# Memory keys and values in three fp32r products; the second norm's scale ahead of the third row pair; GpSimd adds the fourth pair too

## Chip, cores and metric

The kernel runs on one core of a Trainium2 chip, as one program. The metric is the device time of an execution in microseconds; lower is better. TensorE (PE) multiplies, VectorE (DVE), ScalarE (ACT) and GpSimd (POOL) work on tiles in SBUF and PSUM, and SyncE (SP) issues nearly all DMAs.

## What is computed

One layer of a streaming encoder for 512 prompt tokens and 64 sample tokens (T = 576), D = 1024. Three branches (convolution, latent attention, attention into a memory) are gated, summed, projected and normed; a mixture of 32 experts (one group of four, two of its eight experts per token) and a second norm follow. Cut to what matters here:

```python
proj = x @ w_in        # GLU input | q latent | kv latent + rotary key | memory queries | gates
mem_k = (mem_prompt @ w_mem_k).reshape(n_p, n_mem, MEM_HEADS, MEM_HEAD_DIM)   # 256 memory tokens, 4 heads of 128
mem_v = (mem_prompt @ w_mem_v).reshape(n_p, n_mem, MEM_HEADS, MEM_HEAD_DIM)
y_mem = mem_attend(mem_q, mem_k, mem_v)                # softmax(q k / sqrt(128)) v
merged = gates[0] * y_conv + gates[1] * y_mla + gates[2] * y_mem
x1 = layer_norm(DEEPNORM_ALPHA * x + merged @ w_out, g_ln1, b_ln1)
y = hier_moe(x1, ...)                                  # sum of two weighted experts per token
x2 = layer_norm(DEEPNORM_ALPHA * x1 + y, g_ln2, b_ln2)
```

## The kernel before

The program is written by hand, engine by engine: each engine has one list of instructions that it works off in order, and waits on semaphores. A tensor is kept with features on the partitions and tokens along the row.

**Products in three fp32r parts.** The projections of x (weights of 1024 x 128, one "job" each) aren't multiplied in plain fp32. Of a weight item, ACT makes the high part (`high_parts`, L1205; fp32r copy, L1214) and DVE or POOL the low part (`low_part`, L506; subtraction, L512); PE forms high x high, high x low of x, low x high (`product`, L746; matmuls L757). A job on 576 tokens has 8 x 3 x 2 = 48 matmuls of 288 columns. `SPLIT` (L96) lists the items treated like this. They sit in two buffers, `WH[n % 2]` and `WL[n % 2]`; ACT makes part n when the job of part n - 2 is done. `LOW_BY_DVE` (L504) says whose low part DVE makes; POOL makes the others. In the stretch in question these are all DVE's, and POOL has no arithmetic from 17 to 225 us.

**Order of the first stage on PE.** Eight GLU jobs, q0 to q2, kv0, kv1, mq0 to mq3 (memory queries), then kr (rotary key, L801, plain fp32, from `x_raw`). Then plain fp32 again: memory key mk0 (L740, 8 matmuls of 256 columns, `memT` moving), kr_sum (L818), mk1, the sums of squares q_ss and kv_ss (L770), mk2, mk3. Then the memory values: mv_0 to mv_3, each two of eight contraction blocks, 16 matmuls of 512 columns in all (L836); ahead of mv_3 four score products of the memory attention (L781). After that come 20 units of memory attention (4 heads, 5 token tiles): per unit scores, row maximum on DVE (L1589), exponent on ACT (L1282), normalising on DVE (L1596, L1597), two turns on PE (L852), their copy on ACT (L1270), values on PE (L872). The first turn also waits until ACT has moved both value tiles out of PSUM (L1304). Accumulation uses four pairs of PSUM banks; job i takes the pair of job i - 4 (`PAIR`, `BEFORE`, L74) and waits until that one is read.

**Order on DVE.** With each job DVE makes one low part and then seven taps of the convolution (L1522: a product with a scalar and an add, input and accumulator both in SBUF, 576 elements; 124 in all). After mq3's low part come three adds (L1554 to L1556) of squares, 26 taps (7 of the list and 19, L1558), the wait for the root that ACT takes of q_ss (L1256), a reciprocal (L1560), three products, a second reciprocal (L1566) and four products, the rotary key (L1576 to L1580), and then the row maxima of the memory attention, with a tap after every second unit.

**Loads.** Weight items run through a ring of three slots of 1024 columns (`ring`, `ITEMS`, L84); SP loads item i when item i - 3 is released (`released`, L481): by its low part if it is split, by its last use on PE otherwise.

**The tail.** An expert stage gathers rows, multiplies and scatters results; the last three stages stay on the chip as `late_hi` and `late_lo` (L1446, L1885) and are added by one-hot matmuls (L1188). Both expert rows of a token tile come back from DRAM as a pair (`yab`, L689). For tiles 0 and 1 (`N_PAIRED`) POOL adds the pair (L2145), for tiles 2 to 4 PE adds the second row by an identity product (L1179). DVE adds both to the sum (L1976, one input from PSUM), ACT takes variance and root (L1487 to L1491), DVE norms with `lnbc_2` (L1987, L1988), SP writes out (L717). Scale and bias of this norm are loaded ahead of the fifth pair (L687), behind a wait for `e_y`, because an expert's weights lay in their place.

Of the kernel before, what the change touches and what calls it, by code (L numbers as in the profile page):

```python
# [21 lines left out]
D = 1024  # L22
# [64 lines left out]
ITEMS += [(n, 1024, n) for n in ("q0", "q1", "q2", "kv0", "kv1", "mq0", "mq1", "mq2", "mq3")] + [("kr", 256, "kr")]  # L87
# [8 lines left out]
SPLIT = [n for n, _, _ in ITEMS if n != "kr" and n[0] != "u" and n[:2] not in ("mk", "mv")]  # L96
SP_AT = {n: i for i, n in enumerate(SPLIT)}

# [31 lines left out]
N_PAIRED = 2  # L130
# [19 lines left out]
def program(nc, a, o):  # L150

    ctx = ExitStack()
    with ctx:
# [81 lines left out]

        branch = {"z": zT, "om": omT, "ox": oxT}
# [244 lines left out]
        def released(name):  # L481

            if name in SP_AT:
                return (w_lo, SP_AT[name] + 1)
            if name[:3] == "mv_" and name != "mv_3":
                return (mv_used, int(name[3:]) + 1)
            return (job_done, JOB[ITEMS[ITEM[name]][2]] + 1)

# [30 lines left out]
        def _(sp):  # L519
# [205 lines left out]
        def _(pe):  # L725
# [20 lines left out]
            def product(name, it, xh, xl, nk, at=0, first=False, cols=(HT, HT)):  # L746
# [5 lines left out]
                for k in range(nk):  # L752
                    if first:
                        pe.wait_ge(x_lo, k + 1)
                    for w, x in ((WH, xh), (WH, xl), (WL, xh)):
                        for s in range(2):
                            mm = pe.matmul(half(name, s, 128, cols[s]), w[:, n % 2, at + 128 * k:at + 128 * k + 128],  # L757
                                           x[:, k, t0[s]:t0[s] + cols[s]],
                                           start=(k == 0 and w is WH and x is xh), stop=(k == nk - 1 and w is WL))
# [33 lines left out]
            for name in ("q0", "q1", "q2", "kv0", "kv1", "mq0", "mq1", "mq2", "mq3"):  # L793
                proj(name)
# [8 lines left out]
            mm.then_inc(job_done, 1)  # L803
            pe.wait_ge(const_ready, 4)
            pe.wait_ge(in_mem, 48)

            def mem_key(h):
                w = item(f"mk{h}").rearrange("p (k m) -> p k m", k=KT)
                gemm(f"mk{h}", w, lambda k, s: memT[:, k, :], KT, n=MT, halves=1)

            for h in range(MH):
                mem_key(h)
                if h == 0:
                    begin("kr_sum")
                    pe.wait_ge(fold_ready, 1)
                    pe.wait_ge(kr_read, 1)
                    for s in range(2):
                        mm = pe.matmul(half("kr_sum", s, ROPE), fold[:, :], rp[:, 2, HT * s:HT * s + HT], start=True, stop=True)  # L818
                    mm.then_inc(job_done, 1)
                if h == 1:  # L820
                    pe.wait_ge(lat_sum, 2)
                    total("q_ss", 1, sq)
                    total("kv_ss", 1, rp)
            begin("mv0")
            begin("mv1")
            for i in range(4):
# [5 lines left out]
                w = item(f"mv_{i}").rearrange("p (k n) -> p k n", k=2)  # L832
# [339 lines left out]
            for tt in range(NT):  # L1172
# [3 lines left out]
                if tt >= N_PAIRED:  # L1176
# [4 lines left out]
                for n in range(N_LATE):  # L1181
                    if tt == 0:
                        pe.wait_ge(late_rows, 2 * n + 2)
                    for part in (late_hi[n], late_lo[n]):
                        if tt == 0 and part is late_lo[n]:
                            pe.wait_ge(e_yb, N_OUT + n + 1)
                        for h in range(2):
                            mm = pe.matmul(late_bank(tt)[0:nr, h, :], row_hot[:, n, t0:t0 + nr], part[:, 512 * h:512 * h + 512],  # L1188
                                           start=(tt < N_PAIRED and n == 0 and part is late_hi[n]),
# [5 lines left out]
        def _(act):  # L1195
# [9 lines left out]
            def high_parts(upto):  # L1205

                while parts[0] <= SP_AT[upto]:
# [6 lines left out]
                    act.activation(WH[:, n % 2, 0:size], ring[:, i % RING, 0:size], ACT.Copy).then_inc(w_hi, 1)  # L1214
# [24 lines left out]
            for h in range(MH):  # L1239
                if h < 2:  # L1240
                    high_parts(f"mq{h + 2}")
                wait_job(act, f"mq{h}")
                act.activation(split(memq[:, h, :]), both(f"mq{h}"), ACT.Copy, scale=MD ** -0.5).then_inc(mem_proj, 1)
            act.wait_ge(const_ready, 4)
            wait_job(act, "kr")
            act.activation(split(rp[:, 2, :]), both("kr"), ACT.Copy).then_inc(kr_read, 1)

            for h in range(MH):
                wait_job(act, f"mk{h}")
                act.activation(mkT[:, 0, h, :], half(f"mk{h}", 0, 128, MT), ACT.Copy).then_inc(mem_proj, 1)  # L1250
                if h == 0:
                    wait_job(act, "kr_sum")
                    act.activation(split(rp[0:32, 2, :]), both("kr_sum", 32), ACT.Copy).then_inc(kr_read, 1)
                if h == 1:
                    wait_job(act, "q_ss")
                    act.activation(split(norms[:, 0, :]), both("q_ss"), ACT.Sqrt, bias=eps[:, :], scale=1.0 / QL).then_inc(lat_std, 1)  # L1256
                    wait_job(act, "kv_ss")
# [987 lines left out]
```

## Time and profile before

| | |
|---|---|
| median of 3 runs | 859.07 us (857.51 to 860.6) |
| profiled execution | 858.51 us, span 855.6 us |
| PE busy | 793.8 us, 93% |
| DVE, ACT, POOL busy | 44%, 28%, 19% |
| DMA | 172.44 MB, 202 GB/s over the span; 422 to 425 GB/s in most slices from 640 us |
| granted TensorE clock, mean | 0.972 of full speed |

The page gives for each engine the busy time over the whole span, and the same in 40 slices. A share over the span says little about one stage: DVE is at 44% in the mean and at 9 tenths in several slices between 43 and 128 us. So the views that count are the chain of waits (work followed back from the last instruction), the timelines of single engines, and the busy time in chosen stretches. A matmul on fp32 data stands in the records as two, so counts of plain products are doubled there; the last instruction of a group also shows its way through the array (0.3 us), so the distance between starts is the better price.

### The profile page before, as it was taken

What the parts mean: (1) busy time and instruction counts of PE and PEld (TensorE: products, weight loads), DVE (VectorE), ACT (ScalarE), POOL (GpSimd) and SP (SyncE); (2) the same over time, 40 slices, a digit from 0 to 9 for tenths busy, and PEclk for the clock granted to TensorE, in tenths of its full rate; (3) what the DMA queues carried; (4) which work ended last, traced back from release to release, by engine and by line L of the source; (5) the groups of instructions that cost most, each with busy time, mean ns of one, the idle gap of its engine ahead of it and who ended that gap; (6) DMA issues with size and microseconds to landing.
All of it is one profiled execution on the core that took longest, in us unless ns stands there. A gap on an engine that the chain in (4) does not pass through costs nothing.

```text
span 855.6 us, 12244 instructions
## 1 busy us (share of the span) xinstructions
PE 793.8 (93%) x4884; PEld 581.7 (68%) x4884; DVE 375.0 (44%) x676; ACT 239.4 (28%) x463; POOL 160.7 (19%) x160
## 2 busy tenths in 40 slices
PE   5999999999899999999999999998899989786894
PEld 5999986775465999999999994776333333222242
DVE  4799997866676421011101115657321111111227
ACT  5123312744677622122212232011111000000132
POOL 5000001000411343444344330002101011011020
PEclk9999999999999999999999999999899989998798
DMA  8433224213100463222221209659899999999993
GB/s 320 138 103 97 65 75 148 87 47 62 49 2 1 154 207 97 87 67 82 99 87 62 87 1 386 238 208 402 324 388 422 422 424 424 421 425 423 422 386 124
DMA packets 33427, 172.44 MB, mean 202 GB/s; under 512 B 6350, under 2 KB 6910, under 8 KB 25048
## 3 DMA queue, kind: packets, MB, share of 16 engines
q1 hardware_dynamic: 28888, 161.30, 49.6%
q0 software_dynamic: 4480, 10.34, 3.2%
q8 instruction: 39, 0.64, 0.3%
q14 instruction: 20, 0.16, 0.1%
HBM read 162.07 MB, written 15.20 MB: 207 GB/s over the span
## 4 chain that ended last, share of the span: by engine, by line
PE 73%; DMA 18%; DVE 4%; issue 2%; SPq 2%; ACT 1%; POOL 0%; POOLq 0%; ACTq 0%; DVEq 0%
PE PS L757 40%; DMA expert<-in_w_e 7%; PE PS L960 7%; DMA x_rows<-rows,tabs 6%; PE PS L1093 6%; PE PS L740 5%; PE PS L872 3%; PE PS L785 2%; DMA lnbc<-in_b_ln 2%; PE PS L852 2%; PE PS L836 2%; PE PS L916 1%; SPq L689 1%; DMA rows<-x_rows,tabs 1%; PE PS L1117 1%
## 5 line engine op out<-in xcount | busy, mean ns | idle before, releaser
L757 PE MATMUL PS<-x_hi,w_hi 128*128 128x288 f32 (+2 forms) x656 | 142.0, 298 | 9.9 <-DVE x_lo L1505 9.0
L757 PE MATMUL PS<-x_lo,w_hi 128*128 128x288 f32 (+2 forms) x656 | 141.5, 298 | 0.0
L757 PE MATMUL PS<-x_hi,w_lo 128*128 128x288 f32 (+2 forms) x656 | 141.3, 297 | 0.0
L1093 PE MATMUL PS<-expert,moe_tmp 128*64 128x512 f32 (+2 forms) x576 | 113.1, 635 | 12.8 <-DMA expert<-in_w_e 11.3
L1214 ACT ACTIVATE w_hi<-raw_ring 128x1024 fp32r<-128x1024 f32 (+1 forms) x57 | 57.1, 1001 | 214.4 <-PE PS L757 208.5
L757 PEld LDWEIGHTS PS<-x_hi,w_hi 128*128 128x128 f32 x656 | 106.2, 191 | 10.2 <-POOL w_lo L512 9.0
L757 PEld LDWEIGHTS PS<-x_lo,w_hi 128*128 128x128 f32 x656 | 106.3, 191 | 0.0
L757 PEld LDWEIGHTS PS<-x_hi,w_lo 128*128 128x128 f32 x656 | 106.3, 191 | 0.0
L512 POOL TENSOR_TENSOR w_lo<-raw_ring,w_hi 128x1024 fp32r<-128x1024 f32 (+1 forms) x33 | 70.1, 2124 | 136.2 <-ACT w_hi L1214 136.2
L1522 DVE SCALAR_TENSOR_TENSOR conv_z<-attn_tmp,wdw,conv_z 128x576 f32<-128x576 f32 x120 | 90.6, 814 | 0.3
L1093 PEld LDWEIGHTS PS<-expert,moe_tmp 128*64 128x64 f32 (+2 forms) x576 | 35.9, 135 | 78.3 <-issue 76.4
L1660 DVE TENSOR_TENSOR attn_tmp<-attn_tmp,PS 128x576 f32<-128x576 f32 x24 | 18.1, 754 | 148.7 <-PE PS L757 148.7
L1117 PE MATMUL PS<-expert,moe_tmp 128*32 128x512 f32 (+2 forms) x272 | 56.0, 656 | 3.6 <-DMA expert<-in_w_e 3.6
L1869 DVE TENSOR_TENSOR moe_tmp<-moe_tmp,PS 128x256 f32<-128x256 f32 x15 | 6.3, 422 | 106.7 <-ACT moe_tmp L1414 106.7
L512 DVE TENSOR_TENSOR w_lo<-raw_ring,w_hi 128x1024 fp32r<-128x1024 f32 x24 | 30.4, 1268 | 48.3 <-ACT w_hi L1214 47.9
L1117 PEld LDWEIGHTS PS<-expert,moe_tmp 128*32 128x32 f32 (+2 forms) x272 | 16.2, 138 | 33.6 <-issue 33.6
L1414 ACT ACTIVATE moe_tmp<-PS 128x256 f32<-128x256 f32 x15 | 5.8, 384 | 117.2 <-PE PS L1093 117.2
L1589 DVE TENSOR_REDUCE nb<-PS 128x1 f32<-128x256 f32 (+5 forms) x60 | 27.8, 464 | 20.5 <-PE PS L785 13.3
L2102 POOL DMA_INDIRECT rows<-x_rows,tabs x12 | 12.1, 1009 | 128.6 <-DMA x_rows<-rows,tabs 112.7
L1890 DVE SCALAR_TENSOR_TENSOR rows<-PS,w_slot,rows 128x1024 f32<-128x1024 f32 x12 | 15.4, 1284 | 43.3 <-PE PS L1117 43.3
L1043 PE MATMUL PS<-ident,rows 128*128 128x128 f32 x120 | 18.0, 298 | 15.6 <-DMA rows<-x_rows,tabs 12.1
L1043 PEld LDWEIGHTS PS<-ident,rows 128*128 128x128 f32 x120 | 14.2, 150 | 27.0 <-DMA rows<-x_rows,tabs 17.2
(343 smaller groups left out, 1178.2 us busy)
## 6 DMA issues: line engine op xcount, KB each, us to landing
expert<-in_w_e SPq DMA_DIRECT2D x30, 2048.0 KB, 25.2
expert<-in_w_e SPq DMA_DIRECT2D x34, 1024.0 KB, 25.1
raw_ring<-in_w_gate_t SPq DMA_DIRECT2D x24, 512.0 KB, 3.5
raw_ring<-in_w_glu_t SPq DMA_DIRECT2D x8, 512.0 KB, 4.7
raw_ring<-in_w_como_t SPq DMA_DIRECT2D x8, 512.0 KB, 3.6
heads<-in_w_out SPq DMA_DIRECT2D x1, 4096.0 KB, 13.8
x_rows<-x_tiles SPq DMA_DIRECT2D x8, 512.0 KB, 5.4
expert_out<-x_rows SPq DMA_DIRECT2D x8, 512.0 KB, 16.0
```

What stands on the lines that cost most here:

```text
L512: eng.tensor_tensor(WL[:, n % 2, 0:size], ring[:, i % RING, 0:size], WH[:, n % 2, 0:size].bitcast(F32), ALU.subtract).then_inc(w_lo, 1)
L740: mm = pe.matmul(half(name, s, m, n), w[:, k, :], rhs(k, s), start=(k == 0), stop=(k == nk - 1))
L757: mm = pe.matmul(half(name, s, 128, cols[s]), w[:, n % 2, at + 128 * k:at + 128 * k + 128], x[:, k, t0[s]:t0[s] + cols[s]], start=(k == 0 ...
L872: mm = pe.matmul(PS[r * w:(r + 1) * w, 4 + g % 2, 128 * c:128 * c + nr], v, PT[kind][0:nk, n % 4, 128 * j:128 * j + nr], start=(j == 0), s ...
L960: mm = pe.matmul(PS[r0:r0 + nr, 2 * (PAIR[f"c{tt}"]) + s, :], m, w[:, 512 * s:512 * s + 512], start=(k == 0 and n == 0), stop=(k == KT - 1 ...
L1043: mm = pe.transpose(PS[:, k // 4, 128 * (k % 4):128 * (k % 4) + CAP], xg[b][0:CAP, 128 * k:128 * k + 128], ident[0:CAP, 0:CAP])
L1093: mm = pe.matmul(PS[r0:r0 + nr, 2, :].rearrange("p (s f) -> p s f", s=2), xgT[:, k, r0:r0 + nr], w13[s % NB][:, :, k, :], start=(k == 0), ...
L1117: mm = pe.matmul(banks[r0:r0 + nr, h, :], turned[:, j, r0:r0 + nr], w2[s % NB][:, j, 512 * h:512 * h + 512], start=(j == 0), stop=(j == 1))
L1214: act.activation(WH[:, n % 2, 0:size], ring[:, i % RING, 0:size], ACT.Copy).then_inc(w_hi, 1)
L1522: ins = dve.scalar_tensor_tensor(dst, src, wdw[:, c, j:j + 1], dst, ALU.mult, ALU.add)
L1589: dve.tensor_reduce(nb[0:nr, n % 8:n % 8 + 1], PS[0:nr, S_BANK[n % 4], 0:nk], AX.X, ALU.max, negate=True).then_inc(max_done, 1)
L1660: dve.tensor_tensor(split(gate[:, j % 2, n, :]), split(gate[:, j % 2, n, :]), both(f"{name}_{j}"), ALU.mult).then_inc(gate_mul, 1)
```

## The change

Keys and values of the memory are computed like the projections, in three fp32r products. The memory gets a high part `MEM_HI` (ACT, one 128 x 2048 copy) and a low part `MEM_LO` (POOL, one subtraction in place of `memT`). The eight weight items mk0 to mk3 and mv_0 to mv_3 join `SPLIT`: ACT makes their high parts, POOL their low parts (`low_parts("mv_3")`, ahead of its latent outputs). During these eight a third weight buffer is in use (`WH2`, `WL2`; `W_BUF`, `W_PREV`), in the region of `x_raw`. Therefore kr, which reads `x_raw`, moves ahead of mq0, and kr_sum, q_ss and kv_ss move ahead of mk0. In the tail, g_ln2 is loaded ahead of the third pair and b_ln2 ahead of the fourth, and POOL adds the fourth pair (`PAIRED = (0, 1, 3)`).

```diff
@@ jobs and items
-JOBS += ["q0", "q1", "q2", "kv0", "kv1", "mq0", "mq1", "mq2", "mq3", "kr",
-         "mk0", "kr_sum", "mk1", "q_ss", "kv_ss", "mk2", "mk3", "mv0", "mv1"]
+JOBS += ["q0", "q1", "q2", "kv0", "kv1", "kr", "mq0", "mq1", "mq2", "mq3",
+         "kr_sum", "q_ss", "kv_ss", "mk0", "mk1", "mk2", "mk3", "mv0", "mv1"]
...
-SPLIT = [n for n, _, _ in ITEMS if n != "kr" and n[0] != "u" and n[:2] not in ("mk", "mv")]
+SPLIT = [n for n, _, _ in ITEMS if n != "kr" and n[0] != "u"]
 SP_AT = {n: i for i, n in enumerate(SPLIT)}
+W_BUF = {SP_AT["mk0"] + i: 2 - i % 3 for i in range(8)}
+W_BUF = {n: W_BUF.get(n, n % 2) for n in range(len(SPLIT))}
+W_PREV = {n: max((p for p in range(n) if W_BUF[p] == W_BUF[n]), default=None) for n in W_BUF}
...
-N_PAIRED = 2
+PAIRED = (0, 1, 3)
@@ SP, tail
             for tt in range(NT):
                 t0, nr = TILES[tt]
-                if tt == NT - 1:
+                if 2 <= tt < 4:
                     sp.wait_ge(e_y, STAGE_OF[LAST_OF_4] + 1)
-                    for n, name in enumerate(("g_ln2", "b_ln2")):
-                        sp.dma_start(lnbc_2[:, n, :], a[name].broadcast_to([128, D])).then_inc(in_ln, 16)
+                    sp.dma_start(lnbc_2[:, tt - 2, :], a["b_ln2" if tt == 3 else "g_ln2"].broadcast_to([128, D])).then_inc(in_ln, 16)
@@ PE (kr and the sums ahead, as in JOBS)
             for h in range(MH):
-                mem_key(h)
...
+                n = SP_AT[f"mk{h}"]
+                begin(f"mk{h}")
+                pe.wait_ge(w_lo, n + 1)
+                for k in range(KT):
+                    for i, (w, x) in enumerate(((w_high(n), MEM_HI), (w_high(n), MEM_LO), (w_low(n), MEM_HI))):
+                        mm = pe.matmul(half(f"mk{h}", 0, 128, MT), w[:, 128 * k:128 * k + 128], x[:, k, :],
+                                       start=(k == 0 and i == 0), stop=(k == KT - 1 and i == 2))
+                mm.then_inc(job_done, 1)
...
-                        mm = pe.matmul(half(f"mv{m}", 0, 128, 512), memT[:, k, 128 * m:128 * m + 128], w[:, kk, :],
-                                       start=(k == 0), stop=(k == KT - 1))
+                        for r, (x, w) in enumerate(((MEM_HI, w_high(v)), (MEM_HI, w_low(v)), (MEM_LO, w_high(v)))):
+                            mm = pe.matmul(half(f"mv{m}", 0, 128, 512), x[:, k, 128 * m:128 * m + 128], w[:, 512 * kk:512 * kk + 512],
+                                           start=(k == 0 and r == 0), stop=(k == KT - 1 and r == 2))
...
-                if tt >= N_PAIRED:
+                if tt not in PAIRED:
@@ ACT
-                    if n >= 2:
-                        wait_job(act, ITEMS[ITEM[SPLIT[n - 2]]][2])
+                    if W_PREV[n] is not None:
+                        act.wait_ge(*parts_read(SPLIT[W_PREV[n]]))
...
+            act.wait_ge(in_mem, 48)
+            link(act.activation(MEM_HI[:, :, :], memT, ACT.Copy))
+            for h in range(MH):
+                high_parts(("mq2", "mq3", "mk0", "mk1")[h])
+                wait_job(act, f"mq{h}")
+                act.activation(split(memq[:, h, :]), both(f"mq{h}"), ACT.Copy, scale=MD ** -0.5).then_inc(mem_proj, 1)
+
+            high_parts("mk2")
+            wait_job(act, "kr_sum")
...
             for h in range(MH):
                 wait_job(act, f"mk{h}")
                 act.activation(mkT[:, 0, h, :], half(f"mk{h}", 0, 128, MT), ACT.Copy).then_inc(mem_proj, 1)
...
+                high_parts(("mk3", "mv_0", "mv_1", "mv_2")[h])
+            high_parts("mv_3")
@@ POOL
             pool.dma_start(o["conv_sample_T"], U[:, :, PSEG, SEG:SEG + PAD]).then_inc(conv_out, 16)
+            pool.wait_ge(w_hi, SP_AT["mq2"] + 1)
+            link(pool.tensor_tensor(MEM_LO[:, :, :], memT, MEM_HI[:, :, :].bitcast(F32), ALU.subtract))
+            low_parts("mv_3")
             pool.wait_ge(ck_ready, 2)
...
-            for tt in range(N_PAIRED):
+            for tt in PAIRED:
```

## Rows read from the trace of the kernel before

**Rows 1.** Chain of waits, 119 to 156 us: start us, us, what.
```profile
119.32 2.08 PE PS L801 x32
...
121.40 3.65 PE PS L740 x16
...
131.73 6.91 PE PS L740 x32
...
138.63 10.30 PE PS L836 x24
...
150.66 3.45 PE PS L836 x8
...
154.78 0.44 PE PS L852 x2
```

**Rows 2.** Busy time by engine, 100 to 144 us: (x) instructions; clock, DMA share, GB/s.
```profile
100.00:144.00 44.00, 44.00 (x266) 36.55 (x266) 41.50 (x51) 11.46 (x17) 0.00 (x0) 1.00 0.29 89
```

**Rows 3.** Timeline of DVE: start us, us, line, operation, tiles, count [idle before <-releaser].
```profile
101.32 1.23 DVE L512 TENSOR_TENSOR w_lo<-raw_ring,w_hi 128x1024 fp32r<-128x1024 f32 x1
...
111.00 19.04 DVE L1522 SCALAR_TENSOR_TENSOR conv_z<-attn_tmp,wdw,conv_z 128x576 f32<-128x576 f32 x26
...
132.30 3.75 DVE L1560 RECIPROCAL heads<-heads 128x576 f32<-128x576 f32 x1 [2.25 <-ACT heads L1256]
...
149.41 0.86 DVE L1589 TENSOR_REDUCE nb<-PS 128x1 f32<-128x256 f32 x2 [2.54 <-PE PS L781]
```

**Rows 4.** Chain of waits: fp32r products of 288 and of 512 columns.
```profile
99.99 19.34 PE PS L757 x145
...
532.75 8.37 PE PS L960 x35
```

**Rows 5.** Timeline of ACT: high part of mq2, and the third exponent.
```profile
100.22 1.07 ACT L1214 ACTIVATE w_hi<-raw_ring 128x1024 fp32r<-128x1024 f32 x1 [4.08 <-PE PS L757]
...
152.11 0.47 ACT L1282 ACTIVATE heads<-PS,nb 128x256 f32<-128x256 f32 x1 [1.22 <-DVE nb L1589]
```

**Rows 6.** Line 512 on POOL, 285 to 480 us: ns min/median/max, first and last start.
```profile
L512 POOL TENSOR_TENSOR w_lo<-raw_ring,w_hi x27: 1295/2392/2416, 287.8 to 473.5; 128x1024 fp32r<-128x1024 f32 x20, 128x512 fp32r<-128x512 f32 x7
```

**Rows 7.** Timeline of POOL and DVE where both work on SBUF, 5.9 to 309 us.
```profile
5.91 2.35 POOL L512 TENSOR_TENSOR w_lo<-raw_ring,w_hi 128x1024 fp32r<-128x1024 f32 x1 [4.73 <-ACT w_hi L1214]
...
6.91 1.97 DVE L1505 TENSOR_TENSOR x_lo<-x_raw,x_hi 128x576 fp32r<-128x576 f32 x1 [6.91 <-ACT x_hi L1220]
...
9.11 0.64 POOL L2017 TENSOR_TENSOR fold<-ident 128x32 f32<-128x32 f32 x1
...
9.56 1.53 DVE L1505 TENSOR_TENSOR x_lo<-x_raw,x_hi 128x576 fp32r<-128x576 f32 x2
...
306.62 1.42 POOL L2087 TENSOR_TENSOR attn_tmp<-attn_tmp 128x576 f32<-128x576 f32 x1 [5.17 <-DVE attn_tmp L1660]
...
306.95 2.18 DVE L512 TENSOR_TENSOR w_lo<-raw_ring,w_hi 128x1024 fp32r<-128x1024 f32 x1 [0.41 <-ACT w_hi L1214]
```

**Rows 8.** Timeline of the tail: PE's result products, POOL's additions, DVE's sum and norm.
```profile
805.85 3.60 PE L1117 MATMUL PS<-expert,moe_tmp 128*128 128x512 f32 x8
...
824.18 2.37 POOL L2145 TENSOR_TENSOR expert_out<-expert_out 128x1024 f32<-128x1024 f32 x1 [33.25 <-DMA expert_out<-x_rows]
...
826.72 2.40 POOL L2145 TENSOR_TENSOR expert_out<-expert_out 128x1024 f32<-128x1024 f32 x1 [0.17 <-DMA expert_out<-x_rows]
...
828.37 1.22 DVE L1976 SCALAR_TENSOR_TENSOR expert_out<-expert_out,PS 128x1024 f32<-128x1024 f32 x1 [0.90 <-PE PS L1188]
...
835.57 1.28 DVE L1987 SCALAR_TENSOR_TENSOR expert_out<-expert_out,gm,lnbc 128x1024 f32<-128x1024 f32 x1 [3.13 <-DMA lnbc<-in_b_ln]
```

**Rows 9.** Busy time by engine and granted clock (PEclk, behind POOL) in two stretches.
```profile
756.00:759.00 3.00, 2.76 (x16) 0.90 (x20) 0.00 (x0) 0.00 (x0) 0.00 (x0) 0.50 1.00 419
...
155.00:177.00 22.00, 22.00 (x148) 17.76 (x147) 18.77 (x58) 16.77 (x58) 1.09 (x2) 1.00 0.19 67
```

**Rows 10.** Chain of waits in the tail: SP's issue of the third pair.
```profile
812.41 1.51 SPq L689
```

More of the change, by code:

```diff
@@ L86 @@
     ITEMS += [(f"glu_b{_c}", 1024, f"glu_b{_c}"), (f"glu_a{_c}", 1024, f"glu_a{_c}")]
-ITEMS += [(n, 1024, n) for n in ("q0", "q1", "q2", "kv0", "kv1", "mq0", "mq1", "mq2", "mq3")] + [("kr", 256, "kr")]
+ITEMS += [(n, 256 if n == "kr" else 1024, n) for n in ("q0", "q1", "q2", "kv0", "kv1", "kr", "mq0", "mq1", "mq2", "mq3")]
 ITEMS += [(f"mk{i}", 1024, f"mk{i}") for i in range(4)] + [(f"mv_{i}", 1024, "mv1") for i in range(4)]
@@ L792, in _ @@
                 proj(f"glu_a{c}", cols=GLU_A)
-            for name in ("q0", "q1", "q2", "kv0", "kv1", "mq0", "mq1", "mq2", "mq3"):
+            for name in ("q0", "q1", "q2", "kv0", "kv1"):
                 proj(name)
@@ L803, in _ @@
             mm.then_inc(job_done, 1)
+            for name in ("mq0", "mq1", "mq2", "mq3"):
+                proj(name)
             pe.wait_ge(const_ready, 4)
[L805 to L809, printed above, removed]
-            for h in range(MH):
-                mem_key(h)
[L813 to L823, printed above, removed]
+            begin("kr_sum")
+            pe.wait_ge(fold_ready, 1)
+            pe.wait_ge(kr_read, 1)
+            for s in range(2):
+                mm = pe.matmul(half("kr_sum", s, ROPE), fold[:, :], rp[:, 2, HT * s:HT * s + HT], start=True, stop=True)
+            mm.then_inc(job_done, 1)
+            pe.wait_ge(lat_sum, 2)
+            total("q_ss", 1, sq)
+            total("kv_ss", 1, rp)
+            for h in range(MH):
+                n = SP_AT[f"mk{h}"]
[5 more added lines that the diff above has]
+                                       start=(k == 0 and i == 0), stop=(k == KT - 1 and i == 2))
+                mm.then_inc(job_done, 1)
             begin("mv0")
@@ L1188, in _ @@
                             mm = pe.matmul(late_bank(tt)[0:nr, h, :], row_hot[:, n, t0:t0 + nr], part[:, 512 * h:512 * h + 512],
-                                           start=(tt < N_PAIRED and n == 0 and part is late_hi[n]),
+                                           start=(tt in PAIRED and n == 0 and part is late_hi[n]),
                                            stop=(n == N_LATE - 1 and part is late_lo[n]))
@@ L1238, in _ @@
                 act.activation(rp[:, i, :], kvd[:, i, :], ACT.Square).then_inc(lat_sq, 1)
[L1239 to L1243, printed above, removed]
             act.wait_ge(const_ready, 4)
@@ L1246, in _ @@
             act.activation(split(rp[:, 2, :]), both("kr"), ACT.Copy).then_inc(kr_read, 1)
+            act.wait_ge(in_mem, 48)
[6 more added lines that the diff above has]
+            wait_job(act, "kr_sum")
+            act.activation(split(rp[0:32, 2, :]), both("kr_sum", 32), ACT.Copy).then_inc(kr_read, 1)
+            wait_job(act, "q_ss")
+            act.activation(split(norms[:, 0, :]), both("q_ss"), ACT.Sqrt, bias=eps[:, :], scale=1.0 / QL).then_inc(lat_std, 1)
+            wait_job(act, "kv_ss")
+            act.activation(split(norms[:, 1, :]), both("kv_ss"), ACT.Sqrt, bias=eps[:, :], scale=1.0 / KVL).then_inc(lat_std, 1)
+            act.activation(warm[:, :], eps[:, :], ACT.Exp)
             for h in range(MH):
@@ L1250, in _ @@
                 act.activation(mkT[:, 0, h, :], half(f"mk{h}", 0, 128, MT), ACT.Copy).then_inc(mem_proj, 1)
[L1251 to L1257, printed above, removed]
-                    act.activation(split(norms[:, 1, :]), both("kv_ss"), ACT.Sqrt, bias=eps[:, :], scale=1.0 / KVL).then_inc(lat_std, 1)
-                    act.activation(warm[:, :], eps[:, :], ACT.Exp)
+                high_parts(("mk3", "mv_0", "mv_1", "mv_2")[h])
+            high_parts("mv_3")
             def evac_probs(n):
```

28 lines of the change are left out of this document (20 added, 8 removed).

## The prediction

> **What bounds the kernel now.** I read the page first, then the chain of waits, then the stretch that the change touches engine by engine. The page has PE busy nearly all of the span and on most of the chain, so a gain must take TensorE time away where nothing else is late. From 119 to 154 us the chain is PE alone: kr (L801), memory keys (L740), memory values (L836) [rows 1]. Its last row, the first turn of probabilities at 154.78, waited for ACT, which moves the values out: there the stage hands over to the memory attention. The second thing to read is DVE: between 100 and 144 us it is busy 41.50 of 44 us, while POOL does nothing at all [rows 2]. DVE's list of weight subtractions (L512) and convolution taps (L1522) runs without a hole to 130.04, waits 2.25 us for the root, ends at 146.87 and waits 2.54 us for the first scores [rows 3]. So DVE is a second bound with under 5 us of air. From 154.78 the memory attention goes on in step on PE, DVE and ACT, and what follows inherits its shift one for one: projections and gates are PE's, and the expert weights are a DMA stream that starts when PE is done with the gates. The tail is a stage of its own: DVE waits 3.13 us for the second norm's bias at 835.57 [rows 8], then works without a break to the end.
>
> **TensorE's part of the change.** Keys before: 3.65 + 3.65 + 6.91 = 14.2 us; values 10.30 + 3.45 = 13.75 us [rows 1]. After: 4 x 24 products of 256 columns and 48 of 512. An fp32r product of 288 columns costs 19.34/145 = 0.133 us, 6.4 for a projection's 48, and one of 512 columns 8.37/35 = 0.24 us [rows 4]; on the line between these one of 256 is 0.118 us. Keys 96 x 0.118 = 11.3, values 48 x 0.24 = 11.5: PE saves 2.9 + 2.3 = 5.2 us. The product kr (2.08 us) and the three sums only change place.
>
> **What moves with it, if nothing collides.** kr now runs at 93.7 to 95.8, so mq0 ends at 102.2 and ACT's high part of mq2, 1.07 us [rows 5], at 103.3, where DVE was subtracting at 101.32 [rows 3]: DVE waits 2.0 us, its next 33 taps (0.73 us apart, 26 in 19.04) end at 132.0. The sums of squares now run at 122.5 to 124.5, over 7 us before that, so the root is there. The old wait of 2.25 is gone, so DVE's list ends at 146.6, 0.3 us earlier than before. The scores are now ready by 146 and the first row maximum comes at 146.9 in place of 149.41. ACT has the third exponent, whose 152.11 row ends near 152.6 [rows 5], done 2.5 us earlier too, at 150.2, and then moves the two value tiles, 0.6 us each (PE's last value product ended at 154.11, its turn began at 154.78 [rows 1]), so the first turn can start at 151.4 in place of 154.78. So 3.4 of PE's 5.2 us arrive; DVE holds the rest. ACT's added work is nine operations (memory high part 2.0, eight weights 1.07 each): it was busy 11.46 of 44 us [rows 2] and this hides. SP issues the same loads; kr's slot is free at 95.8 and mq2's load (about 3.6 us) lands before 102. The ring slots of keys and values are now freed by POOL's subtraction, always earlier than the use that freed them before. POOL's latent and rotary-key outputs stand behind the new subtractions, but their data come from DVE at 144 or later; the mask loads, which wait for the outputs of memory keys and values, come over 20 us later. ACT's and POOL's copies cost nothing while they keep ahead of PE.
>
> **What POOL's nine subtractions cost.** POOL takes 2.39 us for 128x1024 and 1.30 for 128x512 [rows 6], so 4.6 for the 128x2048 low half of the memory, and 8 x 2.4 for the weights. Against PE they are in time: walked through with a turn between each two DVE operations, the low parts end at 118.0, 121.0, 126.1, 131.9 (keys; needed at 124.9, 127.8, 130.6, 133.5) and 134.9, 137.8, 140.7, 143.7 (values; needed at 136.4, 139.2, 142.0, 146.4). The question is what they do to DVE. Rows show it for one kind of operation. At 306.95 DVE's weight subtraction, which takes 1.23 alone, took 2.18, while POOL's addition of SBUF tiles ran 306.62 to 308.04; at 6.91 DVE's x_lo took 1.97 in place of 0.80, and finished as if started when POOL's 2.35 us subtraction was done [rows 7]. So it isn't a slowdown but a full block: one waits until the other's instruction is over. Blocked time is POOL's duration less about 0.15 to 0.2 (8.07 - 5.91 = 2.16; 307.90 - 306.62 = 1.28 of 1.42), so I price a 1024 subtraction at 2.2 and the memory's at 4.4: 4.4 + 8 x 2.2 = 22.0 us. An operation with one SBUF input and one from PSUM isn't blocked: the sum at 828.37 took 1.22 us in the middle of POOL's addition [rows 8].
>
> All of these nine fall between 104 and 144 us, where DVE does little but taps. Is a tap blocked? No tap of the trace runs beside POOL reading SBUF. The bounds are 0 and 22.0 us. Taps (SCALAR_TENSOR_TENSOR, both tensors in SBUF, 576 elements) start 0.73 us apart [rows 3], x_lo (TENSOR_TENSOR, both in SBUF, 576 elements) too: two cover 1.53 us [rows 7], 0.73 and 0.80. The same reads at the same pace, so I take the value of the blocked kind, 22.0. The Trainium skill, "SBUF — State Buffer", section "Who interferes with whom", says that a VectorE instruction with two SBUF inputs contends with a GpSimd instruction that reads SBUF, and that the later one blocks fully; by that rule the cost is the whole 22.0 us, and a reader who trusts only the rows has 0 to 22.0. The trace agrees for TENSOR_TENSOR and doesn't show taps.
>
> Does POOL get in between back-to-back DVE operations? Its small sum of 32 columns at 9.11 ended at 9.75, just after the x_lo in progress had given way to that of 9.56, while DVE had no gap [rows 7]. So the two engines take turns, and DVE's list slips by all nine.
>
> **The sum of the front.** DVE's list ends at 146.6 + 22.0 = 168.6; small waits that it had anyway take 0.2 off. The first turn comes at 173.2 in place of 154.78: +18.4. PE has finished the values near 149 and stands idle for some 24 us. At 756 to 759, right after PE had waited for weights, the granted clock was 0.50 [rows 9], the lower of the two levels (1.2 and 2.4 GHz). The memory attention has PE busy 22.00 of 22 us at the higher one [rows 9], so half of the slow time is lost: 1.5 us if it is those 3 us, and as much again if it lasts twice as long; I take 1.8. Front: +20.2.
>
> **The tail.** g_ln2 is issued before the third pair and b_ln2 before the fourth, in place of both after it. The wait that guards them asks for the result whose products run from 805.85 to 809.45; SP reaches the third pair at 812.41 [rows 10]: it holds nothing up, and the pairs behind the two loads are only pushed by one and two transfers. Two 512 KB transfers take 2.5 us (POOL's first addition starts at 824.18, the second at 826.72, both on landing [rows 8]). The bias thus lands 2.5 us earlier, at 833.0, the fourth pair 2.5 later, at about 834. PE drops the fourth pair's identity products and is no bound. But POOL now adds the fourth pair, 2.4 us, just when DVE does its norm products with two SBUF inputs: the same block, 2.2 us. Net -0.3; if the bias lands as the earlier work allows (832.5), POOL falls beside the PSUM sum and -2.1 remains. I take -0.9; without any block it would be -2.5.
>
> **Result.** +20.2 - 0.9 = +19.3. The profiled execution took 858.51 us in all (span 855.6); that gives 877.8. The median shown is 0.56 higher: 878.4.
>
> **Rivals.**
> - Taps aren't blocked, only TENSOR_TENSOR is. Then POOL costs DVE at most one weight's 2.3 us at the three sums of squares: front -3.4 + 2.3 = -1.1, tail -2.5: 855.5. For it: no tap is seen beside POOL. Against: reads and pace equal to the blocked form.
> - No collision at all: -3.4 - 2.5 = -5.9, 853.2. Against it stand [rows 7]; it would need that nothing of them carries over to a stretch where DVE is back to back.
> - DVE keeps the lead when back to back, and POOL gets in only beside the two reciprocals (3.75 each, one input) and DVE's last wait. Then the low parts are late for PE: mk0 not before 134 in place of 124.9, the values from 147 on, the first turn near 162: +7.5, less 0.9 in the tail and with the clock kept mostly up: 866. This is slower too, by another wait. Against it: POOL's small sum in [rows 7].
> - The products aren't cheaper (256 columns costing as 512): keys 96 x 0.24 = 23.0, PE 6 us longer in sum; beside a DVE that is 22 us late this is hidden and the time stays 878; without the block it gives +4, 863. The change then doesn't do what it says.
>
> The side flips where POOL's blocking exceeds the 4.3 us that front and tail otherwise gain (3.4 + 0.9): two of the nine subtractions.
>
> **How the numbers follow.** Full block 0.76; DVE first 0.07; taps free 0.10; no collision 0.03; products dear or something unseen 0.04. The likeliest case by itself is 872 to 884: low with 2.16 per subtraction, the clock's loss at 1 us and 2.1 in the tail (876), high with POOL's whole 2.39 and the clock's 3 (882), and some us on either side for the turns. The range takes in the DVE-first case and reaches 865 to 886; what is left out is the side of the gains and a rest, 2 in 10. A difference of 0.3% (2.6 us) is about what measurement can tell from none: faster 0.12, same 0.05, slower 0.83 (full block, DVE first; taps free lies just beyond the border, so it is split).
>
> **What the profile would show.** Keys' products 2.9 us per head, values' 0.24 us each (TensorE part right). POOL busy some 24 us within 103 to 144; taps beside it with up to 3 us where 0.81 stood, the reciprocal at about 154 in place of 132.30, PE idle before the first turn some 24 us with DVE named, granted clock 0.5 just after. In the tail one norm product of about 3.5 us beside L2145's third addition, and less waiting for the bias. If the taps stay at 0.81 beside POOL, the forecast is wrong, and the time falls to 853 to 856. If instead PE waits at the keys for w_lo, POOL is the loser of the turns.

## The result and the profile after

| | before | after |
|---|---|---|
| median (5 runs each, same chip) | 859.07 us (857.51 to 860.6) | 877.76 us (875.69 to 879.09) |
| ratio, 95% interval | | 1.0204 [1.0183, 1.0225] |
| profiled execution, its span | 858.51 us, 855.6 us | 875.69 us, 873.9 us |
| granted TensorE clock, mean | 0.972 | 0.962 |
| first turn of the memory attention | 154.78 us | 172.56 us |
| start of the attention projections | 178.12 us | 197.53 us |
| first sum of the tail on DVE | 828.37 us | 846.87 us |

The changed kernel is 2.0% slower; 878.4 us was forecast. The chain of waits of the changed kernel (start, duration, what), which was TensorE alone in [rows 1], runs through the convolution taps from 104 us on:

```profile
93.99 2.08 PE PS L817 x32
96.06 6.60 PE PS L773 x48
102.77 1.07 ACT w_hi L1234
103.86 1.22 DVE w_lo L529
105.09 6.61 DVE conv_z L1544 x4
...
119.89 31.15 DVE conv_z L1544 x23
...
172.56 0.69 PE PS L872 x2
```

The timeline of DVE in the changed kernel, to be held against [rows 3], where the same 26 taps took 19.04 us and the reciprocal stood at 132.30:

```profile
103.86 1.22 DVE L529 TENSOR_TENSOR w_lo<-raw_ring,w_hi 128x1024 fp32r<-128x1024 f32 x1 [2.35 <-ACT w_hi L1234]
105.00 9.54 DVE L1544 SCALAR_TENSOR_TENSOR conv_z<-attn_tmp,wdw,conv_z 128x576 f32<-128x576 f32 x7
...
117.05 2.84 DVE L1578 TENSOR_TENSOR heads<-heads 128x576 f32<-128x576 f32 x1
119.81 34.07 DVE L1544 SCALAR_TENSOR_TENSOR conv_z<-attn_tmp,wdw,conv_z 128x576 f32<-128x576 f32 x26
153.81 3.74 DVE L1582 RECIPROCAL heads<-heads 128x576 f32<-128x576 f32 x1
```

And the timeline of POOL beside it, the nine subtractions:

```profile
103.91 5.63 POOL L2076 TENSOR_TENSOR mem_lo<-heads,mem_hi 128x2048 fp32r<-128x2048 f32 x1 [36.59 <-ACT w_hi L1234]
115.85 6.29 POOL L529 TENSOR_TENSOR w_lo<-raw_ring,w_hi 128x1024 fp32r<-128x1024 f32 x2 [6.30 <-DVE w_lo L529]
124.16 3.03 POOL L529 TENSOR_TENSOR w_lo<-raw_ring,w_hi 128x1024 fp32r<-128x1024 f32 x1 [2.01 <-ACT w_hi L1234]
130.10 14.41 POOL L529 TENSOR_TENSOR w_lo<-raw_ring,w_hi 128x1024 fp32r<-128x1024 f32 x5 [2.92 <-ACT w_hi L1234]
```

How to read the two together: beside the memory's subtraction seven taps took 9.54 us; seven taps by themselves take 5.19 (shown further down), so 4.35 us were lost there. The add at 117.05 took 2.84 where the same add takes 0.76 when nothing runs beside it (shown further down too): 2.08 lost. The 26 taps took 34.07 for 19.04: 15.03 lost. In sum 21.46 us for nine subtractions, so the loss is spread over many short steps. A view by busy time doesn't show it, since a blocked instruction counts as busy; this is the table of busy time by engine of the changed kernel (columns as in [rows 2]; PEclk is the figure behind POOL):

```profile
100.00:144.00 44.00, 43.62 (x303) 40.90 (x303) 41.61 (x29) 18.28 (x24) 28.14 (x9) 1.00 0.36 118
144.00:170.00 26.00, 5.83 (x27) 4.56 (x25) 25.52 (x33) 1.02 (x4) 2.95 (x5) 0.66 0.13 41
170.00:175.00 5.00, 2.44 (x10) 2.15 (x11) 3.66 (x11) 2.81 (x9) 1.09 (x2) 0.50 0.24 90
175.00:180.00 5.00, 5.00 (x33) 4.41 (x33) 3.64 (x12) 3.12 (x12) 0.00 (x0) 0.86 0.31 121
```

DVE is busy 41.6 of 44 us as before, but with 29 instructions in place of 51. From 149.8 to 172.56 TensorE has nothing to do, and the memory attention then starts at the lower clock (0.50).

### The profile page after: what moved, and what is told of

The parts are those of the page before. It is cut to its first block, busy times and chain, and to the rows that moved or that the text cites. A ratio compares the mean times of both kernels' runs of the same rounds, so it can differ in the third digit from the quotient of the medians.

```text
span 873.9 us, 12367 instructions
## 1 busy us (share of the span) xinstructions
PE 787.4 (90%) x4928; PEld 584.8 (67%) x4928; DVE 397.3 (45%) x676; ACT 248.7 (28%) x472; POOL 191.9 (22%) x170
## 4 chain that ended last, share of the span: by engine, by line
PE 64%; DMA 19%; DVE 11%; issue 2%; ACT 1%; SPq 1%; POOL 1%; POOLq 0%; ACTq 0%; DVEq 0%
PE PS L773 37%; DMA x_rows<-rows,tabs 11%; PE PS L980 6%; DVE conv_z L1544 5%; PE PS L756 3%; DMA expert<-in_w_e 3%; PE PS L1113 3%; PE PS L892 3%; PE PS L801 2%; PE PS L1137 2%; DMA lnbc<-in_b_ln 2%; PE PS L872 2%; PE PS L936 1%; DMA rows<-x_rows,tabs 1%; SPq L705 1%
## 5 line engine op out<-in xcount | busy, mean ns | idle before, releaser
L1234 ACT ACTIVATE w_hi<-raw_ring 128x1024 fp32r<-128x1024 f32 (+1 forms) x65 | 65.4, 1007 | 215.7 <-PE PS L773 207.6
L529 POOL TENSOR_TENSOR w_lo<-raw_ring,w_hi 128x1024 fp32r<-128x1024 f32 (+1 forms) x41 | 93.2, 2272 | 148.1 <-ACT w_hi L1234 141.1
L1113 PE MATMUL PS<-expert,moe_tmp 128*64 128x512 f32 (+2 forms) x576 | 109.4, 612 | 12.6 <-DMA expert<-in_w_e 11.1
L1544 DVE SCALAR_TENSOR_TENSOR conv_z<-attn_tmp,wdw,conv_z 128x576 f32<-128x576 f32 x120 | 109.9, 972 | 0.3
L1063 PEld LDWEIGHTS PS<-ident,rows 128*128 128x128 f32 x120 | 12.9, 141 | 28.5 <-DMA rows<-x_rows,tabs 19.3
## 6 DMA issues: line engine op xcount, KB each, us to landing
expert<-in_w_e SPq DMA_DIRECT2D x34, 1024.0 KB, 10.5
```

The lines of the kernel that those rows point to most:

```text
L529: eng.tensor_tensor(w_low(n)[:, 0:size], ring[:, i % RING, 0:size], w_high(n)[:, 0:size].bitcast(F32), ALU.subtract).then_inc(w_lo, 1)
L1063: mm = pe.transpose(PS[:, k // 4, 128 * (k % 4):128 * (k % 4) + CAP], xg[b][0:CAP, 128 * k:128 * k + 128], ident[0:CAP, 0:CAP])
L1113: mm = pe.matmul(PS[r0:r0 + nr, 2, :].rearrange("p (s f) -> p s f", s=2), xgT[:, k, r0:r0 + nr], w13[s % NB][:, :, k, :], start=(k == 0), ...
L1234: act.activation(w_high(n)[:, 0:size], ring[:, i % RING, 0:size], ACT.Copy).then_inc(w_hi, 1)
L1544: ins = dve.scalar_tensor_tensor(dst, src, wdw[:, c, j:j + 1], dst, ALU.mult, ALU.add)
```

## The experiments

Each was timed beside the kernel before on its own chip, whose median was 860.81 us for the first four and 861.21 for the others; so the ratios count, not the bare times.

### Undo the tail: all of the loss is in the front

```diff
-PAIRED = (0, 1, 3)
+PAIRED = (0, 1)
@@ SP, tail
-                if 2 <= tt < 4:
+                if tt == NT - 1:
                     sp.wait_ge(e_y, STAGE_OF[LAST_OF_4] + 1)
-                    sp.dma_start(lnbc_2[:, tt - 2, :], a["b_ln2" if tt == 3 else "g_ln2"].broadcast_to([128, D])).then_inc(in_ln, 16)
+                    for n, name in enumerate(("g_ln2", "b_ln2")):
+                        sp.dma_start(lnbc_2[:, n, :], a[name].broadcast_to([128, D])).then_inc(in_ln, 16)
```

> The changed kernel with its tail put back (both loads of the second norm ahead of the fifth pair, GpSimd adding two pairs). The prediction put +20.2 on the front and -0.9 on the tail; the trace of the changed kernel has +18.5 us already at the first sum of the tail and +18.4 at the end, so the tail seems worth 0.1. Theory (all of it is in the front): 877 to 879 us, first turn of probabilities at 172.5. Rival (the tail hides a gain of its own that the block takes back, or it is the tail that costs): under 875 if the tail cost something, 880 if it really gave 2.5.

Measured: 880.99 us, ratio 1.0235 [1.0214, 1.0255]; first sum of the tail at 850.09, end at 878.7. The ratio makes 879.3 us of a kernel before of 859.07, just above the 877 to 879 expected. The front alone carries the loss, and the old tail makes it rather larger: with 1.0204 [1.0183, 1.0225] for the whole change the tail is worth about 0.3%, though the two intervals overlap.

### The tail alone, and its loads alone

```diff
@@ kernel before, SP (both experiments)
-                if tt == NT - 1:
+                if 2 <= tt < 4:
                     sp.wait_ge(e_y, STAGE_OF[LAST_OF_4] + 1)
...
@@ first experiment only
-N_PAIRED = 2
+PAIRED = (0, 1, 3)
...
```

> The kernel before with only the tail of the change: scale and bias loaded ahead of pairs three and four, GpSimd adding the fourth pair. Theory: the bias lands only some 1.4 us earlier and GpSimd's third addition blocks a norm product of DVE by 1.3 us, so -0.1 to -0.3: 858.4 to 859.0, with DVE's first norm product waiting about 1.8 us in place of 3.13 and the second taking 2.6 in place of 1.28. Rival (the prediction's term): -0.9, 858.2; rival without any block: -2.5, 856.6. As times these lie close together; the distance from the first tail sum on DVE to the end of the span is what tells them apart.

> The kernel before with only the two loads of the second norm moved ahead of pairs three and four; GpSimd still adds two pairs, PE adds the other three. Theory (the addition on GpSimd is what takes the gain back): -1.4 us, 857.7, the norm product waiting 1.8 us in place of 3.13 and none of the norm products longer than 1.3 us. Rival (the bias's landing is set by something else, so the loads bring nothing by themselves): 859.1, unchanged. Rival (the pushed pairs now come late for PE): above 859.5, with DVE's late sums waiting for the pair.

Measured: 858.98 us, ratio 0.9982 [0.9964, 1.0000], and 859.98 us, ratio 0.9983 [0.9966, 1.0000]. Both ratios are a gain of 0.2% with an interval that reaches to none. The traces tell more. DVE in the kernel with the tail alone (timeline):

```profile
830.17 1.28 DVE L1986 SCALAR_TENSOR_TENSOR expert_out<-expert_out,gm,lnbc 128x1024 f32<-128x1024 f32 x1 [0.31 <-DMA lnbc<-in_b_ln]
...
833.63 1.22 DVE L1975 SCALAR_TENSOR_TENSOR expert_out<-expert_out,PS 128x1024 f32<-128x1024 f32 x1 [0.86 <-PE PS L1187]
834.97 2.42 DVE L1986 SCALAR_TENSOR_TENSOR expert_out<-expert_out,gm,lnbc 128x1024 f32<-128x1024 f32 x1
```

The wait for the bias is down from 3.13 [rows 8] to 0.31; the theory had put it at 1.8, from the one trace of the changed kernel. When the bias lands varies: with the new tail DVE waits 0.24 to 1.93 us for it in six traces of this study and not at all in the seventh (the kernel in which DVE makes the low parts), with the old tail 3.13 and 4.60 in the two. In its place the third sum waits 0.86 for TensorE, and one norm product is held up by POOL's third addition, 2.42 in place of 1.28. From the first sum to the end of the span it is 26.37 us, 0.86 less than in the kernel before (27.23): nearer to the prediction's term of -0.9 than to the -0.1 to -0.3 of the theory. About half of the 0.86 of waiting is the pushed third pair, which TensorE's timeline shows landing 0.41 us late:

```profile
828.85 1.98 PE L1178 MATMUL PS<-expert_out,ident 128*128 128x512 f32 x4 [0.41 <-DMA expert_out<-x_rows]
```

With the loads alone there is no such block, but the chain of waits and the timelines of TensorE and of DVE in that kernel show another limit:

```profile
839.23 1.98 PE PS L1178 x4
841.22 2.76 PE PS L1187 x12
```

```profile
839.23 1.98 PE L1178 MATMUL PS<-expert_out,ident 128*128 128x512 f32 x4 [0.21 <-DMA expert_out<-x_rows]
```

```profile
839.06 1.22 DVE L1975 SCALAR_TENSOR_TENSOR expert_out<-expert_out,PS 128x1024 f32<-128x1024 f32 x1 [0.85 <-PE PS L1187]
...
844.02 1.22 DVE L1975 SCALAR_TENSOR_TENSOR expert_out<-expert_out,PS 128x1024 f32<-128x1024 f32 x1 [1.01 <-PE PS L1187]
...
848.78 1.21 DVE L1975 SCALAR_TENSOR_TENSOR expert_out<-expert_out,PS 64x1024 f32<-64x1024 f32 x1 [0.82 <-PE PS L1187]
```

Per row tile TensorE needs 1.98 + 2.76 = 4.74 us with an identity product, DVE 3.85 (in the kernel before, its first norm products of the first three tiles start that far apart). As soon as the bias is there in time, the third, fourth and fifth sum wait for TensorE, 2.7 us together, and nearly all of the gain of the loads is gone: 27.06 us from the first sum to the end, 0.17 less than before. So the expected 1.4 us didn't come. The third rival of that run (pushed pairs come late for PE) explains the smaller part: TensorE waited 0.22 us for the third pair and 0.21 for the fourth (the row at 839.23; the chain of waits reaches it from that transfer). The other 2.2 us are TensorE's own pace, which no rival of that run named. POOL's addition of the fourth pair is what takes TensorE out of this chain, and costs 1.1 us of block for it.

### GpSimd busy at the same places, but not reading SBUF

```diff
@@ changed kernel, POOL
-            link(pool.tensor_tensor(MEM_LO[:, :, :], memT, MEM_HI[:, :, :].bitcast(F32), ALU.subtract))
-            low_parts("mv_3")
+            link(pool.memset(MEM_LO[:, :, :].bitcast(F32), 0.0))
+            link(pool.memset(MEM_LO[:, :, :].bitcast(F32), 0.0))
+            for n in range(SP_AT["mk0"], SP_AT["mv_3"] + 1):
...
+                link(pool.memset(w_low(n).bitcast(F32), 0.0))
+                pool.memset(w_low(n).bitcast(F32), 0.0).then_inc(w_lo, 1)
```

> The changed kernel, but each of GpSimd's nine subtractions is replaced by two fills with zeros of the same tile, so GpSimd is busy for about as long and at the same place, and reads nothing from SBUF; the low parts of the memory and of its eight weights are zero, everything else is as in the changed kernel. Theory (GpSimd's reading of SBUF blocks DVE's taps and subtractions): the block goes, 7 taps take 5.2 us and 26 take 19.0 as before, first turn near 151.5, 853 to 857 us in all. Rival (GpSimd being busy at all, or semaphores and the order on PE and ACT, make DVE late): taps stay at 9.5 and 34 us and the time at 877.

Measured: 857.71 us, ratio 0.9955 [0.9938, 0.9971]. Timelines of DVE and of POOL in this kernel:

```profile
105.59 5.19 DVE L1544 SCALAR_TENSOR_TENSOR conv_z<-attn_tmp,wdw,conv_z 128x576 f32<-128x576 f32 x7
...
113.43 0.76 DVE L1578 TENSOR_TENSOR heads<-heads 128x576 f32<-128x576 f32 x1
114.10 19.04 DVE L1544 SCALAR_TENSOR_TENSOR conv_z<-attn_tmp,wdw,conv_z 128x576 f32<-128x576 f32 x26
```

```profile
104.47 1.81 POOL L2076 MEMSET mem_lo<- 128x2048 f32 x1 [36.57 <-ACT w_hi L1234]
106.34 1.81 POOL L2077 MEMSET mem_lo<- 128x2048 f32 x1
```

The taps are back at 5.19 and 19.04 to the hundredth, with POOL busy at the same places, if for less time (18.9 us of fills, where the nine subtractions would take about 23.7 by themselves, by [rows 6]); the first turn comes at 151.84. The waits, TensorE's products and ACT's added work are those of the changed kernel, so none of them is the cause. This kernel, whose low parts are zeros, also shows what the change would be worth if they came for nothing: 0.45%, or 3.9 us, where the prediction's terms without the block of the taps (-3.4 and -0.9) give 4.3.

### Copies: one SBUF operand is enough

```diff
@@ the same places, against the kernel with the fills
-                link(pool.memset(w_low(n).bitcast(F32), 0.0))
+                link(pool.tensor_copy(w_low(n), w_high(n).bitcast(F32)))
```

> The changed kernel, but each of GpSimd's nine subtractions is replaced by two copies of the high part, so GpSimd reads one SBUF operand in place of two, for about as long; the low parts of the memory and of its eight weights are wrong by that, everything else is as in the changed kernel. Theory A (any reading of SBUF by GpSimd blocks a tap of DVE): taps beside a copy are held up by that copy's length, 7 taps take over 8 us and the total stays between 872 and 880. Theory B (only GpSimd's instructions with two SBUF operands block): taps at 5.2 and 19.0 us as with the fills, 857 to 859.

The memory's two fills are copies too; the low parts of this kernel are copies of the high parts.

Measured: 873.2 us, ratio 1.0170 [1.0125, 1.0216]. DVE's timeline, then POOL's:

```profile
105.40 8.46 DVE L1544 SCALAR_TENSOR_TENSOR conv_z<-attn_tmp,wdw,conv_z 128x576 f32<-128x576 f32 x7
...
116.37 1.47 DVE L1578 TENSOR_TENSOR heads<-heads 128x576 f32<-128x576 f32 x1
117.77 30.81 DVE L1544 SCALAR_TENSOR_TENSOR conv_z<-attn_tmp,wdw,conv_z 128x576 f32<-128x576 f32 x26
```

```profile
119.27 1.04 POOL L2081 CAST w_lo<-w_hi 128x1024 fp32r<-128x1024 f32 x1 [0.52 <-POOL w_lo L2082]
...
123.93 1.58 POOL L2081 CAST w_lo<-w_hi 128x1024 fp32r<-128x1024 f32 x1 [2.11 <-ACT w_hi L1234]
125.58 1.45 POOL L2082 CAST w_lo<-w_hi 128x1024 fp32r<-128x1024 f32 x1
```

Theory A holds: a GpSimd instruction that reads a single SBUF operand blocks the taps too (3.27 and 11.77 us lost). Each of the sixteen copies of a weight costs DVE 0.78 us (0.71 at the add, which took 1.47 for 0.76, and 11.77 at the 26 taps), and the shortest copy took 1.04. So the block is again the length of the instruction less about 0.25, as with the subtractions (2.14 of 2.39). Together with the fills this is what the Trainium skill, "SBUF — State Buffer", section "Who interferes with whom", says: a VectorE instruction with two SBUF inputs contends with a GpSimd instruction that reads SBUF, not with one that only writes it. The runs agree with both halves: 26 taps take 30.81 us beside copies and 19.04 beside fills.

### DVE makes the low parts itself

```diff
@@ DVE; POOL's nine subtractions are gone
+                if item == "mq2":
+                    link(dve.tensor_tensor(MEM_LO[:, :, :], memT, MEM_HI[:, :, :].bitcast(F32), ALU.subtract))
...
-            taps(19)
+            for name, n in (("mk0", 1), ("mk1", 8), ("mk2", 7), ("mk3", 2), ("mv_0", 2), ("mv_1", 2), ("mv_2", 2), ("mv_3", 2)):
+                low_part(dve, SP_AT[name])
+                taps(n)
```

> The changed kernel, but DVE makes all nine low parts itself (its 1024-column subtraction takes 1.15 us from start to start, so 8 x 1.15 + 2.2 = 11.4 us more on its list), between the same taps, and GpSimd does no arithmetic there. Theory (each GpSimd subtraction holds DVE up for its own whole length, 21.5 us in all): giving the work to GpSimd cost more than doing it; first turn at -3 + 11.4 = +8.4, some 163, total 866 to 868. Rival (DVE's lateness comes from the longer chain of waits among high and low parts, not from the block): 876 to 880 here too.

Measured: 869.44 us, ratio 1.0122 [1.0076, 1.0168]. DVE's timeline and the chain's row of the first turn:

```profile
105.73 2.28 DVE L1575 TENSOR_TENSOR mem_lo<-heads,mem_hi 128x2048 fp32r<-128x2048 f32 x1
108.05 5.20 DVE L1544 SCALAR_TENSOR_TENSOR conv_z<-attn_tmp,wdw,conv_z 128x576 f32<-128x576 f32 x7
...
116.43 1.22 DVE L529 TENSOR_TENSOR w_lo<-raw_ring,w_hi 128x1024 fp32r<-128x1024 f32 x1
```

```profile
163.25 0.69 PE PS L872 x2
```

DVE does the memory's low half in 2.28 us, and lost 4.35 us to the same work on POOL; it does a weight's in 1.14 from start to start and lost 2.14. The first turn is at 163.25 (163 was expected) in place of 172.56: the whole job handed to a second engine cost DVE nearly twice what doing it costs. By its ratio the kernel is 10.5 us slower than before, with an interval of 6.5 to 14.5 that takes in the 7 to 9 expected.

### TensorE kept busy while it waits

```diff
@@ changed kernel, PE, ahead of the memory attention
+            pe.wait_ge(in_route, 32)
+            for _ in range(44):
+                pe.matmul(PS[:, 5, 0:KT * 36], ones[:, :], wr[:, :, :].rearrange("p k e -> p (k e)"), start=True, stop=True)
             pe.wait_ge(mem_proj, 10)
```

> The changed kernel with 44 extra products of 288 columns into an unused bank, which TensorE works on in the stretch where it has nothing else to do, ahead of its wait for the first scores. Theory (the slow clock at the start of the memory attention comes from TensorE having stood idle for some 20 us): the granted clock is near 1 from 172 to 178 us, the stage is 1.5 us shorter, 876.1 where the changed kernel had 877.8. Rival (the clock falls for another reason, or the slow spell has no effect because DVE sets the pace there): no change, 877.8.

Measured: 877.36 us, ratio 1.0211 [1.0169, 1.0252]; the time can't tell a gain of under 2 us here, the trace can. The extra products run from 150.41 to 171.91. Busy time by engine of this kernel, columns as above:

```profile
170.00:175.00 5.00, 3.62 (x20) 2.67 (x20) 4.24 (x13) 3.25 (x12) 1.49 (x3) 1.00 0.15 45
175.00:180.00 5.00, 5.00 (x38) 4.52 (x37) 4.66 (x15) 3.61 (x13) 0.00 (x0) 1.00 0.47 183
```

DVE's low part of mq2 in its timeline:

```profile
104.61 1.23 DVE L529 TENSOR_TENSOR w_lo<-raw_ring,w_hi 128x1024 fp32r<-128x1024 f32 x1 [2.35 <-ACT w_hi L1237]
```

The granted clock is 1.00 where it was 0.50 and 0.86. Counted from that low part (103.86 in the changed kernel) the first turn (172.56, here 173.29) comes after 68.70 us there and 68.68 here, the projections behind the attention (197.53, here 196.63) after 93.67 and 92.02: 1.65 us less, all of it inside the attention. TensorE's idle stretch was the cause of the slow start.

### A version that beats both

Only the keys in three products; two weight buffers as before; DVE makes the five low parts, POOL none; ten taps are left for the idle time after the memory attention; tail as changed.

```diff
-SPLIT = [n for n, _, _ in ITEMS if n != "kr" and n[0] != "u"]
+SPLIT = [n for n, _, _ in ITEMS if n != "kr" and n[0] != "u" and n[:2] != "mv"]
@@ DVE
-            taps(19)
+            for h, n in enumerate((1, 8, 5, 2)):
+                taps(n)
+                low_part(dve, SP_AT[f"mk{h}"])
```

> Only the memory keys in three fp32r products; values stay plain; DVE makes the low half of the memory and of the four key weights (6.8 us more on its list), GpSimd nothing; ten taps of the convolution, 7.3 us, are left for after the memory attention, where DVE stood idle for over 5 us; tail as in the change. Theory (TensorE and DVE both have to be kept on time, GpSimd kept out): keys end 2.5 us earlier, first turn at 152.2, tail -0.9: 855 to 857. Rival (DVE's list is late all the same, since its slack was only 4.8 us): first turn near 155, 859 or more.

Measured: 856.71 us (855.34 to 858.45, 10 runs), ratio 0.9958 [0.9940, 0.9976]: 0.42% faster than before, and so 2.4% faster than the change. Its chain of waits:

```profile
95.18 2.08 PE PS L813 x32
97.26 25.78 PE PS L769 x192
...
126.27 5.75 PE PS L835 x48
132.02 5.99 PE PS L835 x48
138.01 10.30 PE PS L850 x24
...
154.16 0.44 PE PS L866 x2
```

The chain is TensorE alone again. Counted from the start of kr, here 95.18, the first turn comes after 58.98 us; in the kernel before kr would have stood behind kv1, at 119.32 [rows 1] less 192 products of 19.34/145 us [rows 4], which is 93.71, so 61.07. The front gives 2.1 us (2.6 expected, a first turn at 152.2). That kr started at 95.18 here is the scatter of the projections ahead of it: among the kernels that differ from the one before in their tail alone, kr started 1.1 us apart.

## Why the prediction was right

**TensorE's part: right.** Keys start at 125.30 and values at 137.02, so the keys take 11.7 us (11.3 forecast), 0.12 us per product of 256 columns. Values end at 149.8; without the four scores, 1.73, that is 11.1 us (11.5). The rival of dear products is out. The walk without collision forecast a first turn at 151.4; the kernel with fills has it at 151.84, and that in an execution whose kr started at 94.57, where the walk had 93.7.

**Taps are of the blocked kind, at full length: right.** This was the open choice, between 0 and 22.0 us, and 22.0 was taken because taps read as the blocked form does and at the same pace [rows 3, 7]. 21.46 us were lost: 4.35 for the memory (4.4 forecast), 17.11/8 = 2.14 per weight (2.2). The fills show that it is the reading, and nothing else in the change. The root's reciprocal came at 153.81 (154 forecast), the first turn at 172.56 (173.2), TensorE's wait before it was 22.7 us (24).

**Who wins the turn: right.** POOL got in between back-to-back taps every time, and its low parts were on time: TensorE shows no wait at the keys or values. The rival in which DVE keeps the lead is out. POOL paid as well: the five subtractions at 130.10 took 2.88 each, against 2.39 alone [rows 6].

**The clock: right in kind, 1.8 forecast, 1.65 measured.** The start of the projections moved by 19.41 us, the first turn by 17.78; the difference of 1.63 is this term, and the kept-busy kernel gets it back.

**The tail: the size held in the mean, the mechanism was only half seen.** The term was -0.9. From the first sum to the end of the span the two old tails took 27.23 and 28.61 us, the seven new ones 25.82 to 27.59, mean 26.86: -1.1, which rests on only two old tails 1.4 us apart. In the two profiled executions of before and after alone it is 27.23 and 27.03. The row of the bias in the changed kernel, with POOL's third addition and the product that it held up:

```profile
852.66 1.29 DVE L2009 SCALAR_TENSOR_TENSOR expert_out<-expert_out,gm,lnbc 128x1024 f32<-128x1024 f32 x1 [1.76 <-DMA lnbc<-in_b_ln]
...
856.51 2.58 DVE L2009 SCALAR_TENSOR_TENSOR expert_out<-expert_out,gm,lnbc 128x1024 f32<-128x1024 f32 x1
```

```profile
855.61 2.39 POOL L2170 TENSOR_TENSOR expert_out<-expert_out 128x1024 f32<-128x1024 f32 x1 [6.99 <-DMA expert_out<-x_rows]
```

Three steps were off. The bias landed 1.4 us earlier in the changed kernel (5.79 us after the first sum in place of 7.20), not 2.5; the other new tails gained 1.2 to 3.1. The block was priced at 2.2 us and was 0.7 to 1.8: POOL starts during the sum before, or just ahead of it; that sum has one input in PSUM and isn't blocked, and only the rest of its addition falls on the norm product. And "PE drops the fourth pair's identity products and is no bound" missed that TensorE is a bound for the third tile as soon as the bias is on time (0.86 us, of which 0.41 is the pushed third pair), and would be for the others without that very edit. The term's size was near, but by errors that offset each other.

**What the sum left out.** Forecast +19.3, measured +18.7 between the medians and +18.3 between the two spans (+17.2 between the profiled executions' own times). From the start of the projections to the first sum of the tail the sum had nothing; there the ten traces of this study take 647.7 to 652.9 us, the kernel before 650.25, the changed one 649.34. Most of this scatter of 5 us isn't tied to an edit, as two kernels that are the same up to the tail show (647.7 with the whole new tail, 652.2 with the loads alone): it is larger than every term but that of the block, and it is why the terms were checked by distances within a trace. In the change it happened to give 0.9 back. Between the two traces the front was 0.8 smaller than forecast, the tail's gain 0.7 smaller, and this stretch gave 0.9 that nobody had forecast. So the mechanism and its large term were right, and that the sum came within 1 us is in part luck.

## What to carry to other kernels

An engine that is idle isn't free to use: before work goes from VectorE to GpSimd, look whether VectorE is running instructions with two SBUF inputs back to back at that time, and price each GpSimd instruction that reads SBUF at its whole own duration on VectorE's list; here that was 2.14 us for work that VectorE does in 1.14. Where VectorE has little slack, look instead for VectorE work that can wait until a later idle stretch (ten taps moved here), and take only that part of TensorE's saving that the lists can feed. When a transfer is taken out of a chain, compare the per-tile time of the next two engines before counting the gain.

## What the runs showed of the hardware that was not expected

TensorE's clock also falls after short waits, and not each time. In the stage of the latent attention it waits 1.9 us for ACT in every kernel; these are the rows of TensorE's timeline for the same eight products behind that wait, first in the kernel with the loads alone, then in the one with the tail alone, which are the same program up to the tail:

```profile
211.05 5.37 PE L915 MATMUL PS<-raw_ring,proj_tmp 128*128 128x512 f32 x8 [1.93 <-ACT heads L1324]
```

```profile
209.92 3.67 PE L915 MATMUL PS<-raw_ring,proj_tmp 128*128 128x512 f32 x8 [1.93 <-ACT heads L1324]
```

The same work takes 1.7 us more in one of them, with a granted clock of 0.66 from 211 to 216 us. Six of the ten traces have 5.37 there and four 3.67. The changed kernel has 3.67, but shows such a spell later, from 254 to 264 us (clock 0.83), behind a wait of 1.59 us for DVE; the kernel before has none in this stage until its last waits, near 276. So part of the scatter between executions is a spell of the lower clock after a wait of under 2 us that comes or doesn't. What decides it stays open; no run here took that wait away.
